# Block 1 of a two-block transformer kernel: half of the depthwise convolution's taps on GpSimd in two operations each

## The reference, cut to what matters

```
def conv_module(u, conv_w, conv_b, ln_g, ln_b):
    """u: (B,S,2*CONV_WIDTH) -> (B,S,CONV_WIDTH)"""
    a, gate = jnp.split(u, 2, axis=-1)
    y = a * jax.nn.sigmoid(gate)
    y = jnp.pad(y, ((0, 0), (CONV_KERNEL - 1, 0), (0, 0)))
    y = lax.conv_general_dilated(y, conv_w[:, None, :], (1,), 'VALID',
                                 dimension_numbers=('NWC', 'WIO', 'NWC'),
                                 feature_group_count=CONV_WIDTH) + conv_b
    y = layer_norm(y) * ln_g.astype(jnp.float32) + ln_b.astype(jnp.float32)
    return jax.nn.silu(y).astype(u.dtype)
```

## Time and profile before

| What | Value |
|---|---|
| median of 3 runs | 3483.49 us (3480.84 to 3483.56) |
| the profiled execution, its own time | 3477.82 us |
| its span, first to last instruction | 3476.0 us |
| PE busy | 3376.4 us, 97% |
| DVE busy | 1655.5 us, 48% |
| ACT busy | 1227.3 us, 35% |
| POOL busy | 197.8 us, 6% |

### The profile page before, as it was taken

The page is one execution under the profiler, slowest core; times in us unless marked ns, Lnnn a source line. Parts: engine busy times, 40 slices in busy tenths (PEclk is TensorE's granted clock), DMA queues, the critical chain, the costliest instruction groups (busy, mean ns, idle before and its releaser), DMA issues.

```text
span 3476.0 us, 42142 instructions
## 1 busy us (share of the span) xinstructions
PE 3376.4 (97%) x15726; PEld 2639.4 (76%) x15726; DVE 1655.5 (48%) x2158; ACT 1227.3 (35%) x1831; POOL 197.8 (6%) x247
## 2 busy tenths in 40 slices
PE   8989999999999999999998999999999999999998
PEld 6657888775688877888775688887888776678887
DVE  6755443566444344443545554434443543654433
ACT  4343122432422233232444442224222444542233
POOL 1200000011000000000002310000000001300000
PEclk9999999999999999999999999999999999999999
DMA  6213322221233232333220143333332321033332
GB/s 168 67 43 86 97 97 97 85 85 43 69 102 97 97 103 73 96 97 97 73 64 24 30 104 97 97 97 91 96 96 97 85 73 32 16 89 97 97 97 67
DMA packets 434262, 288.19 MB, mean 83 GB/s; under 512 B 44528, under 2 KB 412316, under 8 KB 433896
## 3 DMA queue, kind: packets, MB, share of 16 engines
q1 hardware_dynamic: 431272, 280.02, 27.7%
q0 software_dynamic: 2736, 4.58, 0.9%
q10 hardware_dynamic: 144, 2.10, 0.2%
HBM read 284.53 MB, written 2.13 MB: 82 GB/s over the span
## 4 chain that ended last, share of the span: by engine, by line
PE 92%; DVE 3%; ACT 3%; issue 2%; DMA 0%; DVEq 0%; SPq 0%; ACTq 0%
PE bank L1974 27%; PE bank L1976 26%; PE bank L1975 26%; PE bank L2003 2%; PE bank L2090 1%; PE bank L2136 1%; PE bank L2112 1%; PE bank L2213 1%; PE bank L2180 1%; PE bank L2480 1%; PE bank L2482 1%; PE bank L2042 1%; PE bank L1991 1%; PE bank L1992 0%; PE bank L1995 0%
## 5 line engine op out<-in xcount | busy, mean ns | idle before, releaser
L1974 PE MATMUL bank<-hh,whi 128*128 128x512 f32 x2768 | 1100.8, 398 | 14.3 <-DVE G L1666 6.4
L1975 PE MATMUL bank<-hl,whi 128*128 128x512 f32 x2768 | 1079.7, 390 | 0.0
L1976 PE MATMUL bank<-hh,wlo 128*128 128x512 f32 x2768 | 1079.5, 390 | 0.0
L1374 DVE TENSOR_TENSOR wlo<-raw,whi 128x1024 fp32r<-128x1024 f32 (+2 forms) x534 | 642.7, 1205 | 315.8 <-ACT whi L929 301.2
L929 ACT ACTIVATE whi<-raw 128x1024 fp32r<-128x1024 f32 (+2 forms) x534 | 546.3, 1034 | 258.3 <-PE bank L1976 257.8
L1974 PEld LDWEIGHTS bank<-hh,whi 128*128 128x128 f32 x2768 | 521.3, 188 | 148.5 <-issue 41.5
L1975 PEld LDWEIGHTS bank<-hl,whi 128*128 128x128 f32 x2768 | 521.5, 188 | 113.0 <-issue 7.4
L1976 PEld LDWEIGHTS bank<-hh,wlo 128*128 128x128 f32 x2768 | 520.9, 188 | 109.6
L1974 PE MATMUL bank<-fshi,whi 128*128 128x512 f32 (+1 forms) x1358 | 526.3, 388 | 2.5 <-ACT G L1069 1.6
L1975 PE MATMUL bank<-fslo,whi 128*128 128x512 f32 (+1 forms) x1358 | 522.2, 385 | 0.0
L1976 PE MATMUL bank<-fshi,wlo 128*128 128x512 f32 (+1 forms) x1358 | 522.1, 384 | 0.0
(11 more groups left out here) (250 smaller groups left out, 2526.7 us busy)
## 6 DMA issues: line engine op xcount, KB each, us to landing
raw<-in_ffn_w_gate SPq DMA_DIRECT2D x88, 512.0 KB, 3.8
raw<-in_ffn_w_up SPq DMA_DIRECT2D x88, 512.0 KB, 3.8
raw<-in_ffn_w_down SPq DMA_DIRECT2D x88, 512.0 KB, 3.5
raw<-in_w_in SPq DMA_DIRECT2D x78, 512.0 KB, 3.9
raw<-in_w_up SPq DMA_DIRECT2D x64, 512.0 KB, 4.0
raw<-in_w_down SPq DMA_DIRECT2D x64, 512.0 KB, 3.4
raw<-in_w_out SPq DMA_DIRECT2D x16, 512.0 KB, 4.0
raw<-in_w_in SPq DMA_DIRECT2D x18, 256.0 KB, 3.5
```

Source lines behind the costliest of these rows:

```text
L1374: dve.tensor_tensor(slot3(wlo, s, m), slot3(raw, s, m), slot3(whi, s, m).bitcast(F32), ALU.subtract).then_inc(c.lo_done.sem, 1)
L1974: pe.matmul(o, wh, ah, start=start, stop=False)
L1975: pe.matmul(o, wh, al, start=False, stop=False)
L1976: return pe.matmul(o, wl, ah, start=False, stop=stop)
```

## The change

The 31 taps of channel tile 0 stay on DVE as they were. The 31 taps of channel tile 1 go to POOL. Tap 0 is one operation there. Each of the other 30 is two: a product into a scratch tile, and an addition onto the accumulator. The scratch tile is MIX + 5 x 512, so ACT's move of `rg0` to that place waits until the last far tap is done, and `cmean` on PE waits for both halves. POOL no longer runs through its 12 weighings alone: its taps stand between them in the order of the row. Each of the two operations of a tap waits for the one before it through a semaphore (`far_taps`, `far_part`).

```diff
@@ gpsimd
-                for j in range(n1):
+                def weighed(j):
                     st = stat[:, j % 4, :]
                     pool.wait_ge(c.rcp.sem, c.rcp.at(l, j + 1))
                     for head in HEADS:
...
+                def far_tap(k):
+                    y_, acc, wk = g(A_Y + YW + k), g(A_SG + S), prm[:, P1_CW + TAPS + k:P1_CW + TAPS + k + 1]
+                    if k == 0:
+                        made = b1["groups"]["ca1"]
+                        pool.wait_ge(c.prm_in.sem, c.prm_in.at(l, 7))
+                        pool.wait_ge(c.evac(made).sem, c.emptied(l, made))
+                        pool.tensor_scalar(acc, y_, wk, prm[:, P1_CB + 1:P1_CB + 2], ALU.mult, ALU.add).then_inc(c.far_taps.sem, 1)
+                    else:
+                        pool.wait_ge(c.far_taps.sem, c.far_taps.at(l, k))
+                        pool.tensor_scalar(g(MIX + 5 * S), y_, wk, None, ALU.mult).then_inc(c.far_part.sem, 1)
+                        pool.wait_ge(c.far_part.sem, c.far_part.at(l, k))
+                        pool.tensor_tensor(acc, acc, g(MIX + 5 * S), ALU.add).then_inc(c.far_taps.sem, 1)
+                for s in b1["steps"]:
+                    if s[0] == "weigh" and s[1] >= EXP_LAG:
+                        weighed(s[1] - EXP_LAG)
+                    elif s[0] == "taps":
+                        far_tap(s[1])
@@ scalar
                 elif kind in ("fm", "uq"):
+                    if gr["name"] == "rg0":
+                        act.wait_ge(c.far_taps.sem, c.far_taps.at(l, TAPS))
@@ vector
-            def taps(c, l, a, z):
-                for k in range(a, z):
-                    for t in range(2):
...
+            def tap(c, l, k):
+
+                y_, acc, wk = g(A_Y + k), g(A_SG), prm[:, P1_CW + k:P1_CW + k + 1]
+                if k == 0:
...
+                    ins = dve.tensor_scalar(acc, y_, wk, prm[:, P1_CB:P1_CB + 1], ALU.mult, ALU.add)
+                else:
+                    dve.wait_ge(c.dve_step.sem, c.dve_step.at(l, tap_at[0]))
+                    ins = dve.scalar_tensor_tensor(out=acc, in0=y_, scalar=wk, in1=acc, op0=ALU.mult, op1=ALU.add)
@@ tensor
                 elif kind == "cmean":
                     pe.wait_ge(c.taps.sem, c.taps.at(l, 1))
+                    pe.wait_ge(c.far_taps.sem, c.far_taps.at(l, TAPS))
```

More of the change, by code:

```diff
@@ L85 @@
 SB_AT = [0, 512, 896, 1152]
-ACT_STEPS, DVE_STEPS = (2, 18), (79, 37)
+ACT_STEPS, DVE_STEPS = (2, 18), (48, 37)
 NSA_PAIRS, T_LAG, O_LAG, P_BUFS = 3, 4, 5, 4
@@ L611, in counts_of @@
             c.taps = signal("taps", 1, 0)
+            c.far_taps = signal("far_taps", TAPS, 0)
+            c.far_part = signal("far_part", TAPS - 1, 0)
             n_stick = SB_H // 2 * QT
@@ L1546, in cmp_sum @@
                 dve.tensor_tensor(p_, p_, total.unsqueeze(2).to_broadcast([P, 24, 32]), ALU.mult).then_inc(c.cmp_p.sem, 1)
-            def taps(c, l, a, z):
-                for k in range(a, z):
-                    for t in range(2):
[L1551 to L1568, removed]
+            def tap(c, l, k):
+                y_, acc, wk = g(A_Y + k), g(A_SG), prm[:, P1_CW + k:P1_CW + k + 1]
+                if k == 0:
+                    dve.wait_ge(c.dve_step.sem, c.dve_step.now(l))
+                    dve.wait_ge(c.evac(b1["groups"]["ca0"]).sem, c.emptied(l, b1["groups"]["ca0"]))
+                    ins = dve.tensor_scalar(acc, y_, wk, prm[:, P1_CB:P1_CB + 1], ALU.mult, ALU.add)
+                else:
+                    dve.wait_ge(c.dve_step.sem, c.dve_step.at(l, tap_at[0]))
+                    ins = dve.scalar_tensor_tensor(out=acc, in0=y_, scalar=wk, in1=acc, op0=ALU.mult, op1=ALU.add)
+                if k == TAPS - 1:
+                    ins.then_inc(c.taps.sem, 1)
+                else:
+                    ins.then_inc(c.dve_step.next(), 1)
+                    tap_at[0] = c.dve_step.k
+            tap_at = [0]
             def swap(c, l, gr, bk, evac):
@@ L1784, in _ @@
                     elif s[0] == "taps":
-                        taps(c, l, s[1], s[2])
+                        tap(c, l, s[1])
                     elif s[0] == "mix":
```

## The result

| | median, us | ratio to the kernel before (95% interval) |
|---|---|---|
| before, 12 runs beside it | 3480.73 (3478.36 to 3483.57) | 1 |
| changed, 12 runs | 3486.79 (3483.84 to 3488.94) | 1.0017 (1.0009 to 1.0025) |

The changed kernel is 6.1 us slower, 3 to 9 us by the interval: a loss that is real and lies within the 0.2% called "no change". The forecast was +1 us. The forecast started from three runs of the kernel before; they are among these twelve, and the median of all twelve lies 2.8 us lower, so the change itself is the better comparison.

A forecast was written before the change was run, and what follows sets the result against it. PE was taken to bound the kernel, busy 97% of the span. DVE's relief 0, POOL at 3.3 us a tap 0, plus 1 us for a near stall, on 3483.5, gave 3484.5 us; range 3478 to 3510.

The forecast's parts named there:

- c: Cost of one far tap (product and addition) on POOL: forecast 3.3 us, bounds 1.8 and 5.1.
- the relief: Work leaving DVE in attention: worth 0 us; rival that it shows, 7.4 us faster, chance 0.05.
- The 22.8 us: DVE time leaving per layer: 30 operations of 744 ns plus half of tap 0.
- The addition: Far tap's TENSOR_TENSOR on POOL: taken at 1.3 us, between 0.82 and 3.24.
- the slow row: Profiled POOL TENSOR_SCALAR with one scalar operation on 128 x 512 (L869): 1620 ns, used to bound the tap's operations.
- Both engines reading SBUF: POOL slowed when meeting DVE operations with two SBUF inputs: 0.3 to 0.5 us a meeting, 0.25 us a tap.
- the walk along POOL's row: Taps and weighings followed in POOL's order against PE's transposes: no stall at 3.3 us a tap, three margins 0.4 or less.
- The margins behind weighing 4: POOL's later work ends before it is wanted: margin 1.7 us at weighing 7, 2.5 at `rg0`.
- The signs: Trace marks of a right forecast: POOL busy about 110 of 140 us, no PE wait for POOL over 0.5 us.
- POOL sets the pace above c = 3.73: Rival: PE's transposes wait for weighings in attention; 3504 us at 4.0 a tap, 3560 at 5.1; chance 0.28.
- The rival's formula: PE's delay per layer from weighing 0 to 11 with POOL saturated: 25c - 89.6 us.
- Shutting each other out for whole operations: Rival: DVE and POOL exclude each other from SBUF between tap 0 and `rg0`; 20 us a layer, 3524 us; chance 0.07.

The follow-up runs named there:

- e1: Changed kernel with taps 1 to 30 of channel tile 1 left out altogether, on POOL and DVE; 3481.96 us, ratio 1.0002.
- e7: Changed kernel with both the far products and the weighings written with two scalar operations; 3483.12 us, ratio 1.0007.
- e4: Changed kernel with taps 1 to 30 of channel tile 0 left out on DVE, POOL's work untouched; 3482.43 us, ratio 1.0006.
- e5: Changed kernel with every far tap's product made twice, so three POOL operations a tap; 3575.31 us, ratio 1.0271.
- e3: Changed kernel with the far taps' product written with two scalar operations (times the weight, times 1.0); 3482.43 us, ratio 1.0006.
- e6: Changed kernel with the weighings written with two scalar operations, far taps as they were; 3480.99 us, ratio 1.0000.
- e2: Changed kernel with the same operations, only POOL's order of taps between the weighings altered; 3487.49 us, ratio 1.0016.

## Why the prediction was right, and where its size was off

The measured change lies where the forecast had it, within 0.2%, and what bounds the kernel, the place of the danger and the sign were right. That nothing would stall was wrong. The 1 us that was added for a stall at c = 3.5 was a guess of the right kind and a sixth of the size, and that the absolute times lie only 2.3 us apart (3484.5 and 3486.8) is in part luck, since the kernel before came out 2.8 us lower than the forecast assumed.

**What bounds it, and the relief.** Right. "I cost this at nothing" held twice: in e1 with 20 us less on DVE, and in e7. That the three waits for L1666 were the handing over and not a queue of taps is shown by their standing at 2.6 us in the first layer of every kernel of this study, e4 with its single tap on DVE among them. The 22.8 us were counted too high: operations that stand behind one another overlap, and the earlier trace rows has 42.0 us for 60 taps, 0.70 each and not 0.744. In e1, where POOL's taps are gone too, DVE's busy time is 19.9 us lower than before.

**The product** was taken at 1.55 and is 1.56 to 1.57 undisturbed. **The addition** was taken at 1.3 and is 1.27 to 1.29. **The handshake** was taken at 0.1 and is 0.09 to 0.10 (110.03 minus 108.24 + 1.69 = 0.10). **Tap 0** was taken at 0.8 and took 1.94 in each layer, with nothing waiting for it. A quarter of the figure that the Trainium skill gives for 2048 columns (GPSIMD Engine Reference, section 3.1) was 1.12 us for the addition, an estimate; the trace has 1.27 at its shortest, between that and the 1.62 of the slow row. The quarter is then 0.15 us too low at 512 columns; a fixed part for each instruction would explain it, and no run here measured other widths of this operation.

**Both engines reading SBUF** is the term that was mis-sized, and for the weighings it was left out. Forecast 0.25 us a tap, spread evenly; measured (1815 - 1565) + (1423 - 1270) = 400 ns a tap on average, and not evenly: the taps of the first layer run from 2.9 to 4.9 us. The 0.3 to 0.5 us for a meeting was right for one meeting; it left out that POOL, once held, can be held by the next DVE operation too. The weighings were taken at their old 26.1 us, although POOL now meets DVE in them as well; they took 30.7. In all the meetings cost POOL about 16.7 us a layer (30 x 0.40 + 4.6), where 7.5 were forecast.

The step that failed with it is the walk along POOL's row, from "POOL starts a weighing at the later of its old start and the end of the taps ahead of it" to "So at 3.3 nothing stalls". At weighing 4: "105.1 + 0.8 + 6.6 = 112.5, ends 113.7; wanted at 114.11. Margin 0.4". The 6.6 us were 8.3. At weighing 1, margin 0.1, the two taps took 6.8 us, nearly as forecast, and the weighing 2.79 instead of 1.83. At weighing 3, margin 0.1, the two taps took 7.1 us and the weighing 3.54. With c = 3.42, the measured mean, and the old weighings the same steps give only 0.1 us in a layer; the rest comes from the scatter of the taps around the mean and from the longer weighings.

**The margins behind weighing 4** did not hold either, though no wait for POOL is listed there. Weighing 7 was to end at 147.5, with a margin of 1.7 against 149.16; it ended at 150.76, and the transposes started 0.14 us behind it, at 150.90. PE lists no wait only because the earlier ones had already made it late by as much. Weighing 6 ended at 137.78, where 134.5 was forecast. From weighing 0's start to weighing 7's end POOL took 73.6 us (77.20 to 150.76), and PE had left it 70.2 (78.92 to 149.16). These 3.3 us, less the 0.7 by which weighing 0 was released sooner against PE, are PE's 2.8 us of lateness at weighing 7, within 0.2: in this half of attention POOL set the pace. The end of the row was as forecast: the far taps ended at 206.85 and ACT moved `rg0` at 209.24, 2.4 us later, where 2.5 was forecast.

**The signs.** The addition (1.27 to 1.29), the product (1.57), ACT's move of `rg0` and a tap under 3.6 us came out as the forecast named them. Two signs did not: POOL was busy 129.8 us of the 140 and not about 110 (the forecast's own terms already give 27.7 + 0.8 + 30 x 3.1 = 121.5), and one wait for POOL was 1.26 us, above 0.5.

**The rivals.** POOL sets the pace above c = 3.73: c did not come to that, yet POOL set the pace up to weighing 7, at 3.42 us a tap, because the taps and weighings of that half meet DVE most. The rival's formula was tested in e5 and gave 39 where 42.8 was measured. That PE "does not get such a delay back" held as well: the 3.1 us lost in each layer make 6.2 of the 6.1 us measured (interval 3 to 9). Shutting each other out for whole operations: the truth lies between. In the kernel after, DVE operations that began inside a far addition were held: L1397 took 2.05 us on average (8 of them) instead of 1.22, and the tap 1.27 instead of 0.74 (12 of them). Those that began inside a far product took 1.27 (14 of them) and 0.83 (23 of them). Here one of the first kind, DVE's and then POOL's timeline:

```profile
84.19 2.06 DVE L1397 TENSOR_TENSOR wlo<-raw,whi 128x1024 fp32r<-128x1024 f32 x1
...
83.88 1.29 POOL L888 TENSOR_TENSOR G<-G 128x512 f32<-128x512 f32 x1
```

The DVE operation began 0.3 us into the addition, which ended at 85.17, and ended itself at 86.25, 1.08 us after it, which is nearly its own undisturbed 1.22: it had hardly begun before.

The means for the product hide two kinds. In the five kernels with the one-scalar product, 25 operations of DVE (taps and L1397) began within the first 0.43 us of an undisturbed product, and all were held; 49 began 0.46 us or more into it, and none was. Those held all end at the same place, a tap 0.33 us before the product's end. An example from the changed kernel, DVE's and then POOL's timeline:

```profile
189.29 1.18 DVE L1580 SCALAR_TENSOR_TENSOR G<-G,prm 128x512 f32<-128x512 f32 x1
...
189.24 1.57 POOL L886 TENSOR_SCALAR G<-G,prm 128x512 f32<-128x512 f32 x1
```

So the product keeps DVE out for about its first 0.7 us (an estimate: a tap held by an addition ends 0.55 us behind it, so it begins some 0.2 us before the release; 1.57 - 0.33 - 0.74 + 0.2 = 0.7), and for the remaining 0.9 us it does not. The evidence against this rival in the prediction was a tap that began 0.59 us into a weighing (102.29 and 101.70), which is behind that point. The rule of the Trainium skill (SBUF, State Buffer, "SBUF: two separate sides"), an exclusive lock for the whole instruction, agrees with the trace where POOL's operation has two inputs and where POOL starts second, and disagrees for the one-input product, where the trace shows it for the first 0.7 of 1.57 us only. DVE lost 7.5 us a layer by it (busy 91.54 us of the 140 where e1, with the same row on DVE and POOL free, has 84.07). All but the 0.3 us at L1598 lay beside idle time, and the price that this rival gave, 20 us a layer, did not arise: more than half of each product left DVE through.

**What stays open.** Why each wait of PE costs 0.1 to 0.2 us more than the idle time listed for it was not found. The profiled execution after is 9.2 us longer than the one before, 3 us more than the change; part of that is the clock. The profile after has 11 us more at half of the clock than the one before (90.8 against 79.7, summed over the span). One such stretch stands in its first layer behind attention (granted clock 0.81 from 222 to 240 us, 1.00 before), but it is not the change's: e1, e3, e4, e6 and e7, none of them measurably slower, have 0.81 to 0.91 there, and e2 has 1.00.

## What to carry to other kernels

Work that was moved off an engine with idle time beside it bought nothing here, and its price was set by what stands behind it in the row of the engine that took it: count the consumer's margin at each place, not the engine's free time over the stage. Where two engines slow each other in SBUF, an average cost for a meeting is wrong for a margin of a few tenths; look which stretches of the other engine's row are dense, and count the meetings of the operations that were there before as well (here the weighings, 4.6 us a layer). A consumer without a listed wait need not have had a margin: compare its start with the start in the kernel before. An operation's form can matter more than its arithmetic: here a second scalar operation in the product, which changes no value, took the whole loss away.

## What the runs showed of the hardware

A GpSimd TENSOR_SCALAR on 128 x 512 float32 with one scalar operation takes 1.56 us and with two 0.69 at its shortest (999 ns on average beside DVE's taps; 782 ns as a weighing). The form with less arithmetic is twice as slow. A GpSimd TENSOR_TENSOR addition of that size takes 1.27 us, less than the one-scalar product. GpSimd held back a DVE operation with two SBUF inputs that started inside its addition, by 0.5 to 0.8 us on average. Inside its one-scalar product it held back all 25 that started in the first 0.43 us and none of the 49 that started 0.46 us or more into it: the product takes 1.57 us and blocks DVE for about 0.7 of them. In e5 each of PE's ten waits for POOL of 4.3 us or more came with a stretch at a granted clock of 0.5 that began during the wait or 0.3 us behind it, 7 to 10 us long in nine cases and 3.4 in one. No such stretch began within 60 us of the waits of 0.3 to 1.3 us in the kernel after.
